# A two-block float32 network on one core: 34 products of constants taken out of TensorE's program

## The reference, cut to what matters

```python
cs = silu(c)
for layer in range(2):
    shift, scale, gate = split(cs @ ada_w[layer] + ada_b[layer], 3)
    h = rms_norm(x, norm_g[layer]) * (1 + scale) + shift
    y = even_mixer(h, ...) if layer % 2 == 0 else odd_mixer(h, ...)
    x = x + gate * y
```

## Time and profile before

| | |
|---|---|
| Median of 3 runs | 1304.23 us (1303.8 to 1304.3) |
| The profiled execution's own time | 1304.39 us |
| Its span, first to last instruction | 1302.6 us |
| TensorE busy (products) | 1273.2 us, 98% |
| VectorE busy | 815.7 us, 63% |
| ScalarE busy | 694.5 us, 53% |
| Mean granted TensorE clock | 0.999 |
| DMA, mean rate | 171 GB/s |

### The profile page before, as it was taken

How to read it: one execution, slowest core, us unless ns; L and a number is a source line. 1 busy time by engine, 2 the same in 40 slices (tenths; PEclk the granted TensorE clock), 3 DMA queues, 4 the chain that set the end, 5 groups by cost and what they waited for, 6 DMA issues and landing times.

```text
span 1302.6 us, 24906 instructions
## 1 busy us (share of the span) xinstructions
PE 1273.2 (98%) x10560; PEld 1144.5 (88%) x10560; DVE 815.7 (63%) x1245; ACT 694.5 (53%) x901; POOL 92.4 (7%) x73
## 2 busy tenths in 40 slices
PE   6999999999999999999999999999999999999997
PEld 5998899879999999999888888999999899888885
DVE  4567766876656867666555545556868657555542
ACT  2556546865766565245544435766566235544432
POOL 0000000000002310320000000001330130000000
PEclk9999999999999999999999999999999999999999
DMA  9866756624444443235555554434433125555452
GB/s 386 294 242 263 282 197 240 221 98 163 150 142 160 144 137 112 67 110 182 181 177 191 175 185 159 161 130 162 163 130 131 67 89 186 175 181 194 163 184 74
DMA packets 35102, 222.93 MB, mean 171 GB/s; under 512 B 3888, under 2 KB 8240, under 8 KB 9264
## 3 DMA queue, kind: packets, MB, share of 16 engines
q1 hardware_dynamic: 31248, 216.23, 46.9%
q10 hardware_dynamic: 3744, 5.11, 1.2%
HBM read 220.28 MB, written 1.05 MB: 170 GB/s over the span
## 4 chain that ended last, share of the span: by engine, by line
PE 87%; DVE 7%; ACT 3%; DMA 2%; issue 1%; SPq 0%; ACTq 0%; DVEq 0%
PE pj L630 58%; PE yv L630 14%; PE sc L630 10%; PE tp L630 4%; DVE ring_rounded L744 3%; PE tp L496 1%; DMA ring<-weights 1%; ACT w_split L735 1%; PE tp L1884 1%; DMA xT<-x_t 1%; DVE att_area L573 1%; DVE rw L1672 0%; DVE big L1847 0%; ACT att_area L527 0%; DVE yT_rounded L1839 0%
## 5 line engine op out<-in xcount | busy, mean ns | idle before, releaser
L744 DVE TENSOR_TENSOR ring_rounded<-ring,w_split 128x2048 fp32r<-128x2048 f32 x108 | 253.2, 2348 | 49.3 <-ACT w_split L735 46.8
L735 ACT CAST w_split<-ring 128x2048 fp32r<-128x2048 f32 x106 | 201.6, 1903 | 35.4 <-PE pj L630 24.2
L2110 DVE TENSOR_TENSOR ring_rounded<-ring,big_rounded 128x2048 fp32r<-128x2048 f32 x66 | 151.3, 2292 | 108.9 <-ACT big_rounded L1981 108.8
L630 PE MATMUL pj<-h_split,w_split 128*128 128x256 f32 x1264 | 173.8, 288 | 0.8 <-ACT w_split L2360 0.8
L630 PE MATMUL pj<-h_split,ring_rounded 128*128 128x256 f32 x1264 | 164.4, 280 | 1.1 <-DVE ring_rounded L744 1.1
L630 PEld LDWEIGHTS pj<-h_split,w_split 128*128 128x128 f32 x1264 | 157.6, 191 | 7.7 <-issue 5.9
L630 PEld LDWEIGHTS pj<-h_split,ring_rounded 128*128 128x128 f32 x1264 | 155.2, 188 | 2.6 <-DVE ring_rounded L744 1.9
L1981 ACT CAST big_rounded<-ring 128x2048 fp32r<-128x2048 f32 x66 | 125.8, 1906 | 51.8 <-PE pj L630 50.2
L630 PE MATMUL pj<-hT_rounded,w_split 128*128 128x256 f32 x1136 | 148.0, 283 | 0.0
L630 PEld LDWEIGHTS pj<-hT_rounded,w_split 128*128 128x128 f32 x1136 | 141.5, 192 | 0.0
L1352 POOL TENSOR_TENSOR big<-big 128x512 f32<-128x512 f32 x16 | 30.7, 1919 | 768.0 <-DVE big L1281 759.8
(11 more groups left out here) (366 smaller groups left out, 2155.6 us busy)
## 6 DMA issues: line engine op xcount, KB each, us to landing
ring<-weights SPq DMA_DIRECT2D x180, 1024.0 KB, 4.9
big<-weights SPq DMA_DIRECT2D x20, 1024.0 KB, 7.5
first_block<-biases ACTq DMA_DIRECT2D x26, 192.0 KB, 4.4
first_block<-biases SPq DMA_DIRECT2D x6, 192.0 KB, 11.3
xT<-x_t SPq DMA_DIRECT2D x1, 1024.0 KB, 9.3
out_t<-scr SPq DMA_DIRECT2D x4, 256.0 KB, 2.9
con<-constants SPq DMA_DIRECT2D x1, 897.0 KB, 6.7
aux<-small SPq DMA_DIRECT2D x1, 832.0 KB, 10.7
```

Source lines behind the costliest of these rows:

```text
L630: return nc.tensor.matmul(out, lhsT, rhs, start=start, stop=stop, skip_group_check=True)
L735: act.post(nc.scalar.copy(w_split[:, w % 2], ring[:, in_ring(idx)]), s["w_high"])
L744: dve.post(nc.vector.tensor_tensor(ring_r[:, at], ring[:, at], w_split[:, w % 2].bitcast(F32), ALU.subtract), s["w_low"])
L2110: dve.tell(nc.vector.tensor_tensor(w_low(t, i), w, value(w_high(i)), ALU.subtract), s["ffn_low"])
```

## The change

The helper `pe_turning` and its five calls are deleted. No other engine's program changes, and nothing else of TensorE's.

```diff
-        def pe_turning(bank, n):
-
-            for _ in range(n):
-                matmul(bank[:, 0:P], C("ident"), C("ones"))
-
...
                 pe_slot(pe, f"ada0_{i}")
-                if i == 5:
-                    pe_turning(sc[0], 9)
-            pe_turning(sc[0], 12)
             pe_first_pair(pe, *EVEN_FIRST[:2])
...
             pe_squares(pe, KC // 2 - 1, scr)
-            pe_turning(sc[0], 3)
             pe_sums_by_token(pe)
-            pe_turning(sc[0], 3)
             pe_spread(pe, s["norm_spread"])
-            pe_turning(sc[0], 7)
             for n in ODD_FIRST:
                 pe_slot(pe, n, (s["h_high"], s["h_low"], 1) if n == ODD_FIRST[0] else None)
```

## The result

The change makes the kernel slower by 0.24%: 1307.37 us in the median of 10 runs (1305.84 to 1308.05) against 1304.06 us of the kernel before (1303.77 to 1304.3), a ratio of 1.0024 with a 95% interval of 1.0016 to 1.0033. That is 3.3 us, a little over the 2.6 us (0.2%) that the prediction set as the bound of "the same". The runs also scatter more: over 2.2 us, where those of before lie within 0.5 us. The profiled execution took 1306.91 us, with a span of 1305.1 us.

What follows compares the result with a forecast made beforehand. TensorE, busy 98% of the span, was taken to bound the kernel. 1304.39 - 0.2 direct gain + 1.4 head clock fall = 1305.6 profiled, so 1305.4 us against 1304.23, counted as the same; range 1303.7 to 1308.3.

Steps and rivals of the forecast that it cites:

- the direct gain: Head and norm: time saved by not running the 34 products, clock aside; 0.2 us (0 to 0.3).
- The 9 and the 12: Head: the products after the sixth and after the eighth modulation slot; removing either is worth 0 by itself.
- The head's price: Head: a clock fall costs 1.55 us, 0.18 of it on the wait ahead of 34.52, leaving 1.4 us.
- Covered by the load: Head: a slowed last slot makes `h_split` 0.86 us later, hidden by the load and ScalarE's work before 32.20.
- The step that failed: Head and norm: the clock falls in the head (1.4 us), not at the norm; head alone had 0.37.
- the gap of 3.5 us: Head: TensorE's new idle time after the last slot, up to 32.20 us, expected to let the clock fall.
- The 1.36 us before 22.63: Head, kernel before: idle time between thin slots that left the next slot at 1.08 us, held against "both".
- the rival "both": Clock falls in the head and at the norm: 1.4 + 1.55 - 0.2 = +2.75 us, 1307.0; chance 0.32.
- the signs of being wrong that were named ahead: Low level well over 3 us of dense products, a fall somewhere else, or the load behind 33.3 us moving.
- The price of a fall: Either place: 3.1 us of products at the low clock with half the work done, so 1.55 us.
- The 7: Norm: the products just ahead of the projections; removing them gains about 0.1 us (0 to 0.15).
- the slot behind the 9: Head: the seventh modulation slot may start 0.7 us earlier, at about 25.1, which buys nothing.

Runs made afterwards that it cites:

- norm_again: Repeat of `norm_out`: only the norm's 13 products deleted from the kernel before; 1305.34 us against 1304.16, ratio 1.0009.
- norm_out: Only the norm's 13 products (3, 3 and 7) deleted from the kernel before, the head's 21 kept; 1305.28 us, +1.17 us, ratio 1.0008.
- norm_double: The kernel before with twice as many products at the norm (6, 6 and 14); 1306.61 us against 1304.05, ratio 1.0021.
- half: The kernel before with 18 products instead of 34 (5 and 6 in the head, 2, 1 and 4 at the norm); 1304.00 us against 1304.16.
- after_again: The changed kernel, all 34 products deleted, measured a second time against the kernel before; 1307.37 us against 1304.05, ratio 1.0026.
- threes_out: Only the norm's two calls with 3 products deleted from the kernel before; 1304.00 us against 1304.05, ratio 1.0001.
- nine_out: Only the head's 9 products after `ada0_5` deleted from the kernel before; 1304.56 us, +0.45 us.
- after_third: The changed kernel, all 34 products deleted, measured a third time against the kernel before; 1307.09 us against 1304.16, ratio 1.0023.

## Why the prediction was right or wrong

**What held.** The effect is TensorE's clock and the direct gain is next to nothing. `norm_again` shows it best: the same program as `norm_out`, and without a fall it takes the time of before. The 9 and the 12 cost nothing by themselves: the first projection starts 1.30 us behind the start of ScalarE's cast with all of them (before, `norm_double`), with half (`half`) and with none (31.88 - 30.58, `after_again`). The head's price, 1.4 us, was measured as 1.40 and 1.19 us. "Covered by the load" held too, though by little: `ada0_7` took 1.78 instead of 1.08 us and VectorE's `h_split` began at 31.06 instead of 30.22. The load came 0.6 us earlier than in the profile of before, so that the cast began at 30.28, and the profile now names `h_split` and not the cast as what the projections waited for. They started 1.34 us behind the cast, 0.04 us later than in the others.

**The step that failed** is "I take it that the clock falls in the head and, where gaps are at most 1.6 us, not at the norm". It falls at the norm too. In the changed kernel the gaps there are 0.55, 0.61 and 1.43 us, and at the fall (191.8 us) the last had hardly begun; in `threes_out` it fell behind gaps of 0.55 and 0.61 us alone. `norm_out` and `norm_again` have the same gaps, and one fell and the other did not. So the length of the longest gap does not tell whether the clock falls. In the head `nine_out` fell without the gap of 3.5 us that I had built on. The argument that I had for the head, that thin slots between 6.33 and 12.7 us did not lift the clock, fitted the norm as well, and I dropped it there for the gap rule. The 1.36 us before 22.63, which I held against it, was one gap and not a row of them. What exactly decides on a fall, these runs do not show.

What came true was the rival "both", 1307.0, 0.4 us from the result. The forecast, 1305.4, was +1.2 us where +3.3 was measured; it is the time of either half alone (1305.3 to 1305.5). The range (1303.7 to 1308.3) holds 1307.37 only because it was drawn wide enough for that rival, so the time within it does not speak for the mechanism. "Slower by over 0.2%" had 0.26 and is what the median shows, if only just. One of the signs of being wrong that were named ahead was met too, a low level of well over 3 us of dense products: 5.4 us at the norm.

**Sizes.** The price of a fall was put at half of the low stretch. At the low level more than half of the work is done: a record of 128x256 takes 0.213 us at the low level (15 in 3.20 us), and at the high one 0.118 at the norm and 0.129 in the head (4.14 us for 32 in `norm_double`). The modulation slots of the earlier trace rows had that ratio already, 1.94 to 1.08, 1.8 and not 2. A microsecond of low clock that meets projections therefore costs 0.45 us at the norm (1 - 0.118/0.213), and that gives all four profiles with a fall among the projections there. The loss is taken against the 8.43 us (196.47 - 188.04) of `norm_again`:

| profile | low clock met by projections, us | times 0.446 | measured loss, us |
|---|---|---|---|
| the changed kernel, first | 5.4 | 2.4 | 2.42 |
| `norm_out` | 3.4 | 1.5 | 1.50 |
| `after_again` | 3.1 | 1.4 | 1.35 |
| `after_third` | 3.4 | 1.5 | 1.51 |

The direct gain at the norm was put at 0.2 us; without a fall it is 8.43 us against 8.48, so 0.05. The sums do start sooner, 1.19 us behind the squares instead of 1.34, but 0.10 of it is given back: from the sums to the spreading it is 1.22 us in `norm_again` and 1.12 before. The four records of the sums take 0.61 us in `norm_again`, where they follow an idle stretch, and 0.50 us before, where they follow other products. The 7 cost nothing: from the spreading to the first projection it is 2.14 us without them and 2.15 us with them, where I had put 0.1. In the head I let the slot behind the 9 start 0.7 us earlier, at 25.1. It started at 26.10, waiting for VectorE's `mod_raw`, and at 25.58 and 25.48 in the two later profiles: the length of that gap varies, and nothing hangs on it in the sum.

**The reading between.** The head looked free because the profile of before was a poor reference for it: its weight load came late (`even0`'s cast began at 30.90, in `norm_double` at 30.29, in the changed kernel at 30.28). From the start of `ada0_7` to the products with the low part of the weights it took 8.90 us before (36.50 - 27.60), but 8.13 us in `norm_double` (27.77 to 35.90) with the same head, and 9.18 after (36.93 - 27.75). Of the 1.05 us between the last two, 0.26 is regained behind them, most of it in a wait for VectorE's `ring_rounded` that before has at 42.4 us: from the low part of the weights to the squares it is 151.96 us before (188.46 - 36.50), 151.70 after (188.63 - 36.93). That leaves 0.8 us for a low level that ends at 34.8. Reckoned in the same way it is 1.5 us where it ended at 36.9 (`after_again`, 37.98 - 28.06) and 2.0 us where it ended at 37.5 (`after_third`, 38.20 - 27.80). The loss grows with what the low level covers of the stream of projections, 3.2, 5.0 and 5.7 us in these three. Times 0.39 (1 - 0.129/0.213), less 0.43 us of waits that go with it (the 0.17 us ahead of 33.91 in `norm_double` and the 0.26), that gives 0.8, 1.5 and 1.8 us. What the low level covers differs from profile to profile, which fits the wider scatter of the runs.

**Open.** Why the halves do not add up to the whole (2.4 against 3.0 to 3.3 us). A part may be the runs of the norm's half without a fall: the 9 of 11 above before are at +1.46 and +1.63 us in the mean, and all three profiles of the whole change have the fall at the norm. With these the halves give 2.6 to 2.8 us. That the head's delay moves the norm to a worse position is not what the profiles show: with the squares late, at 189.66 and 189.91 us, the norm lost 1.35 and 1.51 us, and 2.42 with the squares at 188.63. The low level in the head lasted 6.8, 6.8 and 10.2 us in the three profiles of the whole change and 6.8 and 3.4 us in the two of the head's half, but these two were each the fastest of their 11 runs. And no run shows what sets whether and when the clock falls.

## What to carry to other kernels

Where TensorE's work is thin between two dense parts, do not go by the longest gap: here the clock fell with none over 0.61 us at that place, and the dense part behind it ran at the low clock at first and lost 1 to 2.4 us. Products of constants can bridge such a stretch at no cost if they end before the awaited data is there. What goes beyond that is paid for, and after a fall they themselves run slowly and hold up what stands behind them. So put in few (18 did here what 34 did). One profile of each kernel is one draw of such an effect: look at the scatter of the runs first, and take a second kernel with the same code at that place as a reference before calling a stretch free.

## What the runs showed of the hardware that was not expected

- The low stretches had three lengths in the profiles: 3.4 us, 6.8 us and once 10.2 us (27.2 to 37.5).
- The clock fell while TensorE was not idle: in the first profile after it fell at 28.0 us within the products of `ada0_7` (27.75 to 29.5), in `norm_out` at 193.3 us, 0.8 us into the projections (192.49), in `threes_out` at 191.0 us within the spreading (190.59 to 191.4).
- The program of `norm_out` had no fall at all in the profile of `norm_again`, with the clock at 1.00 from 186 to 206 us.
- The low level (1.2 GHz) did not cost half of the pace in these float32 products: 0.213 us a record of 128x256 against 0.118 to 0.129 at the high one (2.4 GHz).
